# Hybrid recurrent and attention block: first projections taken from unnormalised x, and the y projection put ahead of the gates in each step

## Chip, cores and metric

One core of a Trainium2 chip. The metric is the device time in microseconds (us), 1733.96 as the median of three runs of the kernel before (1733.42 to 1734.18). The profile is one further execution: its own time is 1732.49 and its span, first to last instruction, 1730.7. All times inside it are counted from the start of that span. PE is TensorE, ACT ScalarE, DVE VectorE, POOL GpSimd, SP the engine that issues the weight loads.

## What is computed

x is 1024 tokens of 1024 features in float32. The part that the change touches is this (the rest is attention, the gated merge, the output projection and a SwiGLU block):

```python
h = rms_norm(x, norm_pre_mix)                # x / deviation(token) * gain(feature)
lru_u, lru_y, q, k, v, ... = split(h @ w_in) # u and y are 1280 wide each
u = causal_depthwise_conv(lru_u, width=4) + conv_b
r = sigmoid(u_block @ w_rg + b_rg); i = sigmoid(u_block @ w_ig + b_ig)
a = exp(-8 * r * softplus(-lru_lambda)); b = sqrt(1 - a*a) * (i * u)
lru_h[t] = a[t] * lru_h[t-1] + b[t]          # a scan over time
lru_out = lru_h * gelu(lru_y)
```

## The kernel before

Everything lies transposed: features on the 128 partitions, tokens along the free axis. The tokens are done in two halves of 512 (h = 0, 1). A projection makes one output tile of 128 features x 512 tokens from 8 weight tiles; each operand is split in a high and a low part, and three matmuls of 512 columns per weight tile (hi*hi, hi*lo, lo*hi) are summed in a PSUM bank. Lines 424, 425 and 426 are these three in `project`, lines 486 to 488 the same in `head`. Weights come through a ring of four buffers: SP loads a block of four tiles (`load`), POOL splits it in high (L358) and low part (L361), PE uses it. SP may load a block when POOL has split the one four places earlier; POOL may split one when PE is done with the one four places earlier.

Each half starts with the recurrent stage, `recurrent(h)`, which each of PE, ACT and DVE runs as its own instruction stream, in the order written. The ten tiles j of u and y pass through it. Tiles 0 and 1 are projected in `head`. Then comes one step for each j from 2 to 9, with these parts:

- PE: the u projection of tile j into bank 0 (5.5 us of matmuls), the two gate products of tile j-2 into banks 4 and 5 (`gates`, 2 or 3 weight tiles each), the y projection of tile j into bank 2. Bank 0 is free when ACT has copied it out (`u_copied`), bank 2 when ACT has taken the gelu of the last one (`gelu_made`).
- ACT: `conv_in(j)` copies u out of PSUM and makes the first tap (L738 to L747); `lru_out_hi(j-3)` (L791); `gate_fns(j-2)`, two Tanh (L759, L761), an Exp (L766) and a Tanh (L768); `conv_hi(j)` (L752); `gate_root(j-2)`, a Sqrt (L774); `decay(j-2)` (L786); `gelu(j)` (L780). Gelu, Exp and Sqrt lie in three different function tables, and each change of table is an ACT_TABLE_LOAD.
- DVE: `conv(j)`, three multiply-adds (L1155); `lru_out_lo(j-3)` (L1191); `conv_lo(j)` (L1161), which waits for `conv_hi(j)`; then `recurrence(j-2)`: L1167, which waits for the second Tanh, L1170 and L1171, which wait for the Exp and the Sqrt, L1174, the scan L1178, L1182, and the product with gelu, L1185.

After step 9 comes `kvq`: the k projections with the gates of tiles 8 and 9 between them, v, and then the q projections, of which the third may not start before DVE has made the low part of the first (`q_lo`, L1255); DVE makes that after the recurrence of tile 9. In the first half all of this stands behind the start: x tiles are loaded, ACT squares them, DVE sums them (L1422), PE sums over partitions (L436), ACT takes the root, DVE inverts (L1410) and makes a diagonal, PE spreads it (L444), and DVE and ACT make the normalised tiles (`normalise`, L1134 and L1143). 24 turns of two warm-up matmuls (L670) stand ahead on PE. A constant of the recurrence is made by 17 small DVE instructions (`prepare`), between tile 1 and step 2. The order of ACT's instructions in a step is

```python
conv_in(h, j, n + 2, j % 4)
if j > 2:
    lru_out_hi(h, j - 3)
gate_fns(h, j - 2, n + 2)
conv_hi(h, j, j % 4)
gate_root(h, j - 2)
decay(h, j - 2)
gelu(h, j, n + 6, j % 4)
```

Of the kernel before, what the change touches and what calls it, by code (L numbers as in the profile page):

```python
# [65 lines left out]
L_STEP = UNIT + [2, 2] + UNIT + (UNIT + GATE + UNIT) * 3  # L66

L_TAIL = UNIT + [3, 3] + UNIT + [2, 2]
V_BLOCKS = [4, 4, 4, 4]
# [45 lines left out]
def build(nc, x_d, par_d, alibi_d, eye_d, w_d, x1_d, out_d):  # L115
    with ExitStack() as ctx:
# [56 lines left out]
        lru_lo = at("lru_lo", [P, KR, T], F32R)  # L173
        mg_hi = at("mg_hi", [P, KD, T], F32R, reg_b)
# [33 lines left out]
        BK_U, BK_Y = (0, 1), (2, 6)  # L208
# [6 lines left out]
        par_loaded = sem("par_loaded")  # L215
# [92 lines left out]
        def _(sp_eng):  # L308
            def load(dram, g, sizes, n):
                off = 0  # L310
                for b, size in enumerate(sizes):

                    wait_pos(sp_eng, w_lo_made, n + b - RING + 1)
                    sp_eng.dma_start(w_raw[:, b % RING, 0:size * P],
                                     dram[g, :, off:off + size * P]).then_inc(w_loaded[b % RING], 16)
                    off += size * P

            def stream(stages, bases):
                for name, sizes, groups in stages:
                    per = 1 if len(sizes) % RING == 0 else 2  # L320
                    sizes2, dram, base = sizes * per, w_d[name], bases[name]
                    n_it = groups // per
                    first = 1 if base == 0 else 0
                    if first:
                        load(dram, 0, sizes2, 0)
                    if n_it - first == 1:
                        load(dram, first, sizes2, base + first * len(sizes2))
                    elif n_it > first:
                        with sp_eng.Fori(first, n_it) as g:
                            load(dram, g, sizes2, g * len(sizes2) + base)  # L330
# [3 lines left out]
            sp_eng.dma_start(par[:], par_d).then_inc(par_loaded, 16)  # L334
            sp_eng.dma_start(eye[:], eye_d).then_inc(par_loaded, 16)
# [62 lines left out]
        def _(pe):  # L398
# [34 lines left out]
            def narrow_sum(part, start, stop):  # L433

                for m in range(T // P):
                    last = mm(ps[:, m, 0:2], part[:, m * P:(m + 1) * P], ones[:, 0:2],  # L436
# [20 lines left out]
            def gates(h, j, n, size, slot, q, first=None):  # L457
# [9 lines left out]
                if last_tile:  # L467
                    pe.wait_ge(r_made, J)
                    pe.wait_ge(i_made, J)
# [4 lines left out]
            def head(h, j, ready):  # L474

                n = BASE[h]["head"] + 4 * j
                wait_pos(pe, row_out, 2 * (BK_Y[j] + 1) * h)
                for b in range(2):
                    for u, bank in enumerate((BK_U[j], BK_Y[j])):
                        pe.wait_ge(w_lo_made, n + 2 * b + u + 1)  # L480
                        for q in range(4):
                            k, w = 4 * b + q, slice(q * P, (q + 1) * P)
                            if ready:
                                pe.wait_ge(h_lo_made, KD * h + k + 1)
                            s = 2 * b + u
                            mm(ps[:, bank, :], w_hi[:, s, w], h_hi[:, k, :], start=(k == 0), stop=False)  # L486
                            mm(ps[:, bank, :], w_hi[:, s, w], h_lo[:, k, :], start=False, stop=False)  # L487
                            last = mm(ps[:, bank, :], w_lo[:, s, w], h_hi[:, k, :], start=False,  # L488
                                      stop=(k == KD - 1))
                        last.then_inc(blocks_done, 1)  # L490

            def recurrent(h):
                for j in range(2):
                    head(h, j, j == 0)
                if h:
                    stat_sum(2)
                for j in range(2, KR):
                    n, slot = 6 * (j - 2) + BASE[h]["step"], 6 * (j - 2)
                    wait_pos(pe, u_copied, (j + KR * h) * 2)
                    project(0, n, slot, UNIT, h_hi, h_lo)  # L500
                    i = j - 2
                    if i in (0, 4):
                        gates(h, i, n + 2, 2, slot + 2, 0, [(i - (i > 0)) % 4, (i + (i == 0)) % 4])
                    else:
                        gates(h, i, n + 2, 3, slot + 2, i)
                    wait_pos(pe, gelu_made, j + KR * h)
                    project(2, n + 4, slot + 4, UNIT, h_hi, h_lo)
# [163 lines left out]
            pe.wait_ge(summed_0, KD - 1)  # L671
            narrow_sum(acc, True, True)
            spread_rstd(1)
            for h in range(HALVES):
                recurrent(h)
                kvq(h)
                pe.wait_ge(par_loaded, 32)
# [20 lines left out]
        def _(act):  # L698
# [17 lines left out]
            def narrow_deviation(n):  # L716
# [878 lines left out]
```

## Time and profile before

| | |
|---|---|
| median of three runs | 1733.96 us |
| the profiled execution, its time and its span | 1732.49 and 1730.7 us |
| PE busy | 1692.4 us, 98% of the span |
| POOL busy | 1320.2 us, 76% |
| DVE busy | 801.4 us, 46% |
| ACT busy | 561.0 us, 32% |
| TensorE clock granted, mean | 0.991 of full |

A matmul of 512 columns is shown with 0.39 us, but the next one starts 0.23 us later: matmuls are pipelined and their ends are modelled. So PE's waits are read in starts, not in busy time. Shares of the span are means over stages: DVE is at 46% over the span, while in the recurrent stage it hardly rests.

### The profile page before, as it was taken

Reading aid. Unit: us, or ns where it says so; the run is one execution under the profiler, and the core shown is the slowest. Engines: PE = TensorE matmul, PEld = TensorE weight load, DVE = VectorE, ACT = ScalarE, POOL = GpSimd, SP = SyncE. Lnnn points to the kernel's source line nnn. Section 1 sums busy time; section 2 is a strip of 40 time slices with the busy share of each in tenths; the row PEclk is TensorE's granted clock in tenths of the full one; section 3 lists DMA queues with packets and bytes.
Section 4 is the critical chain, followed back from the end, with each engine's and each line's share of the span. In section 5 each row is a group of like instructions: output and inputs, shape, how many; then the busy total and the mean of one; then the engine's idle time right before and its main releaser. Section 6 shows DMA issues by size and latency. Waiting matters only on the chain.

```text
span 1730.7 us, 26755 instructions
## 1 busy us (share of the span) xinstructions
PE 1692.4 (98%) x7676; PEld 1392.5 (80%) x7676; DVE 801.4 (46%) x878; ACT 561.0 (32%) x1034; POOL 1320.2 (76%) x1344
## 2 busy tenths in 40 slices
PE   8999999999999999999999999999999999999995
PEld 6787888888888878888888888888888888888884
DVE  5899736651277987766421733211611232111013
ACT  4577435442236765254422322111200211111000
POOL 5799966777788999777777877776777777666774
PEclk8999999999999999999999999999999999999997
DMA  4333332232343333422323434322433343224331
GB/s 142 102 88 89 116 98 85 79 98 94 108 128 106 90 89 108 155 75 76 96 94 103 140 130 143 109 96 93 137 100 95 111 143 132 94 95 141 96 97 60
DMA packets 111228, 183.15 MB, mean 106 GB/s; under 512 B 12352, under 2 KB 38208, under 8 KB 111168
## 3 DMA queue, kind: packets, MB, share of 16 engines
q1 hardware_dynamic: 97056, 156.15, 29.2%
q10 hardware_dynamic: 14112, 26.22, 4.5%
q8 instruction: 35, 0.57, 0.1%
q14 instruction: 25, 0.20, 0.0%
HBM read 173.94 MB, written 8.39 MB: 105 GB/s over the span
## 4 chain that ended last, share of the span: by engine, by line
PE 86%; issue 5%; POOL 4%; DVE 3%; ACT 1%; DMA 0%; POOLq 0%; ACTq 0%; SPq 0%; DVEq 0%
PE ps L426 27%; PE ps L425 26%; PE ps L424 26%; POOL w_hi L358 3%; POOL w_lo L361 1%; PE ps L486 1%; PE ps L565 1%; PE ps L487 1%; PE ps L488 1%; PE ps L555 0%; PE ps L557 0%; PE ps L556 0%; PE ps L580 0%; PE ps L579 0%; DVE rows L1482 0%
## 5 line engine op out<-in xcount | busy, mean ns | idle before, releaser
L361 POOL TENSOR_TENSOR w_lo<-w_raw,w_hi 128x512 fp32r<-128x512 f32 (+2 forms) x664 | 849.4, 1279 | 55.4
L358 POOL TENSOR_SCALAR w_hi<-w_raw 128x512 fp32r<-128x512 f32 (+2 forms) x664 | 466.5, 703 | 334.2 <-PE ps L426 261.1
L424 PE MATMUL ps<-h_hi,w_hi 128*128 128x512 f32 x1376 | 538.1, 391 | 9.9 <-POOL w_lo L361 7.5
L426 PE MATMUL ps<-h_hi,w_lo 128*128 128x512 f32 x1376 | 541.0, 393 | 0.0
L425 PE MATMUL ps<-h_lo,w_hi 128*128 128x512 f32 x1376 | 538.8, 392 | 0.0
L424 PEld LDWEIGHTS ps<-h_hi,w_hi 128*128 128x128 f32 x1376 | 258.4, 188 | 71.2 <-issue 6.4
L425 PEld LDWEIGHTS ps<-h_lo,w_hi 128*128 128x128 f32 x1376 | 258.4, 188 | 57.3
L426 PEld LDWEIGHTS ps<-h_hi,w_lo 128*128 128x128 f32 x1376 | 258.6, 188 | 54.3
L1122 DVE TENSOR_TENSOR acc<-acc,sq 128x512 f32<-128x512 f32 x55 | 66.3, 1206 | 226.7 <-ACT sq L969 201.7
L1447 DVE TENSOR_TENSOR tmp<-ps,tmp 128x512 f32<-128x512 f32 x44 | 30.4, 691 | 301.8 <-PE ps L426 301.8
L426 PE MATMUL ps<-f_hi,w_lo 128*128 128x512 f32 x352 | 138.7, 394 | 0.0
L425 PE MATMUL ps<-f_lo,w_hi 128*128 128x512 f32 x352 | 138.0, 392 | 0.0
L424 PE MATMUL ps<-f_hi,w_hi 128*128 128x512 f32 x352 | 136.6, 388 | 0.0
L1049 ACT ACTIVATE f_hi<-tmp 128x512 f32 (+1 forms) x44 | 27.8, 633 | 230.8 <-DVE tmp L1447 230.8
L969 ACT ACTIVATE sq<-ps 128x512 f32 (+1 forms) x32 | 19.1, 597 | 225.9 <-PE ps L426 208.0
L1155 DVE SCALAR_TENSOR_TENSOR uc<-u_raw,par,uc 128x512 f32<-128x512 f32 x60 | 71.9, 1199 | 17.9 <-ACT uc L747 16.4
L425 PEld LDWEIGHTS ps<-f_lo,w_hi 128*128 128x128 f32 x352 | 66.1, 188 | 15.5
L424 PEld LDWEIGHTS ps<-f_hi,w_hi 128*128 128x128 f32 x352 | 66.1, 188 | 14.8
L426 PEld LDWEIGHTS ps<-f_hi,w_lo 128*128 128x128 f32 x352 | 66.2, 188 | 13.1
L893 ACT ACTIVATE prob<-prob,stat 128x128 f32<-128x128 f32 x128 | 49.7, 389 | 63.1 <-DVE stat L1276 63.1
L1450 DVE TENSOR_TENSOR f_lo<-tmp,f_hi 128x512 f32 (+1 forms) x44 | 45.0, 1024 | 42.4 <-ACT f_hi L1049 42.4
L1046 ACT ACTIVATE tmp<-ps 128x512 f32<-128x512 f32 x44 | 26.3, 598 | 117.2 <-PE ps L426 117.1
(193 smaller groups left out, 2431.3 us busy)
## 6 DMA issues: line engine op xcount, KB each, us to landing
w_raw<-w_f SPq DMA_DIRECT2D x176, 256.0 KB, 3.0
w_raw<-w_step SPq DMA_DIRECT2D x64, 256.0 KB, 2.6
w_raw<-w_b SPq DMA_DIRECT2D x64, 256.0 KB, 3.0
w_raw<-w_d SPq DMA_DIRECT2D x64, 256.0 KB, 2.7
w_raw<-w_a SPq DMA_DIRECT2D x96, 128.0 KB, 2.0
xs<-x_t ACTq DMA_DIRECT2D x32, 256.0 KB, 3.4
w_raw<-w_q SPq DMA_DIRECT2D x32, 256.0 KB, 3.2
w_raw<-w_o SPq DMA_DIRECT2D x32, 256.0 KB, 3.0
```

The costliest lines, as they stand in the source:

```text
L358: nc.gpsimd.tensor_scalar(w_hi[:, s, w], w_raw[:, s, w], 1.0, 0.0, ALU.mult, ALU.add).then_inc(w_hi_made, 1)
L361: nc.gpsimd.tensor_tensor(w_lo[:, s, w], w_raw[:, s, w], rd(w_hi[:, s, w]), ALU.subtract).then_inc(w_lo_made, 1)
L424: mm(out, w_hi[:, s, w], x_hi, start=(k == 0), stop=False)
L425: mm(out, w_hi[:, s, w], x_lo, start=False, stop=False)
L426: last = mm(out, w_lo[:, s, w], x_hi, start=False, stop=(k == total - 1))
L893: fn(prob[:, i, :], prob[:, i, :], ACT.Exp, bias=stat[:, 2, i:i + 1], accum_out=stat[:, 3, i:i + 1]).then_inc(exped, 1)
L1046: fn(tmp[:, 0, :], ps[:, 0, :], ACT.Silu).then_inc(silu_made, 1)
L1049: fn(f_hi[:, bass.ds(t, 1), :], tmp[:, 1, :], ACT.Copy).then_inc(f_hi_made, 1)
L1122: tt(acc[:], acc[:], sq[:], ALU.add).then_inc(summed, 1)
L1155: stt(uc[:, q, :], u_raw[:, k:k + T], col("conv_w", j + KR * k), uc[:, q, :], ALU.mult, ALU.add).then_inc(taps, 1)
L1447: tt(tmp[:, 1, :], ps[:, 1, :], tmp[:, 0, :], ALU.mult).then_inc(f_made, 1)
L1450: tt(f_lo[:, bass.ds(t, 1), :], tmp[:, 1, :], rd(f_hi[:, bass.ds(t, 1), :]), ALU.subtract).then_inc(f_lo_made, 1)
```

## The change

1. At the start of the first half, `head` projects x times the gain (xg_hi, xg_lo), which ACT and DVE make as the x tiles land, instead of the normalised tiles. The statistics are taken beside it on PE (the narrow sum after the third block, the spreading after the fifth). The reciprocal deviation is multiplied into the results: DVE's `scale_u` and `scale_y` for tiles 0 and 1. The normalised tiles are made after that, for step 2 onwards.
2. The parameters are loaded first, the four first weight blocks between the x tiles, the identity matrix last. `prepare` moves into the start, in two parts.
3. In every step of both halves the y projection goes ahead of the gates, on PE and in the order of the weight blocks (`L_STEP`, `step_offsets`). ACT's order in a step becomes conv_in, lru_out_hi, conv_hi, gelu, gate_fns, gate_root, decay. DVE's order in a step stays.
4. The first step of a half waits for tile 0's copy only, since tile 1 lies in other banks; y of tile 1 of the first half goes to bank 3.

The core of the diff:

```diff
-L_STEP = UNIT + [2, 2] + UNIT + (UNIT + GATE + UNIT) * 3
+L_STEP = UNIT + UNIT + [2, 2] + (UNIT + UNIT + GATE) * 3
...
-        BK_U, BK_Y = (0, 1), (2, 6)
+        BK_U, BK_Y = (0, 1), ((2, 3), (2, 6))
...
+            sp_eng.dma_start(par[:], par_d).then_inc(par_loaded, 16)
             for t in range(KD):
                 sp_eng.dma_start(rows[:, t, :], x_d[0][t]).then_inc(x0_loaded[t], 16)
-            sp_eng.dma_start(par[:], par_d).then_inc(par_loaded, 16)
-            sp_eng.dma_start(eye[:], eye_d).then_inc(par_loaded, 16)
+                if t in (0, 1, 3, 4):
+                    b = (0, 1, 3, 4).index(t)
+                    sp_eng.dma_start(w_raw[:, b, :], w_d["head"][0, :, b * CAP:(b + 1) * CAP])\
+                        .then_inc(w_loaded[b], 16)
+            sp_eng.dma_start(eye[:], eye_d).then_inc(eye_loaded, 16)
...
                         last.then_inc(blocks_done, 1)
+                        if h == 0 and u == 0 and (j, b) == (0, 1):
+                            pe.wait_ge(summed_0, KD - 1)
+                            narrow_sum(acc, True, True, 4)
+                        if h == 0 and u == 0 and (j, b) == (1, 0):
+                            spread_rstd(1)
...
-                    wait_pos(pe, u_copied, (j + KR * h) * 2)
-                    project(0, n, slot, UNIT, h_hi, h_lo)
+                    first = j == 2
+                    pe.wait_ge(u_copied, (j - first + KR * h) * 2)
+                    project(0, n, slot, UNIT, h_hi, h_lo, (h_lo_made, 0) if first and h == 0 else None)
+                    if first and h == 0:
+                        pe.wait_ge(y_scaled, 1)
+                    else:
+                        pe.wait_ge(gelu_made, j - first + KR * h)
+                    project(2, n + 2, slot + 2, UNIT, h_hi, h_lo)
                     i = j - 2
                     if i in (0, 4):
-                        gates(h, i, n + 2, 2, slot + 2, 0, [(i - (i > 0)) % 4, (i + (i == 0)) % 4])
+                        gates(h, i, n + 4, 2, slot + 4, 0, [(i - (i > 0)) % 4, (i + (i == 0)) % 4])
                     else:
-                        gates(h, i, n + 2, 3, slot + 2, i)
-                    wait_pos(pe, gelu_made, j + KR * h)
-                    project(2, n + 4, slot + 4, UNIT, h_hi, h_lo)
+                        gates(h, i, n + 4, 3, slot + 4, i)
...
+            def conv_scaled(j):
+                wait_pos(act, taps, j * 3)
+                fn(u_raw[:, 0:TAPS - 1], u_carry[:, bass.ds(j, 1), :], ACT.Copy).then_inc(u_ctx, 1)
+                act.wait_ge(u_copied, j * 2 + 1)
+                act.wait_ge(u_ctx, j + 1)
+                fn(u_carry[:, bass.ds(j, 1), :], u_raw[:, T:T + TAPS - 1], ACT.Copy)\
+                    .then_inc(u_copied, 1)
+                fn(uc[:, j, :], u_raw[:, 0:T], ACT.Identity, bias=col("conv_b", j),
+                   scale=col("conv_w", j)).then_inc(tap0, 1)
...
                     if j > 2:
                         lru_out_hi(h, j - 3)
-                    gate_fns(h, j - 2, n + 2)
                     conv_hi(h, j, j % 4)
+                    gelu(h, j, n + 4, j % 4)
+                    gate_fns(h, j - 2, n + 4)
                     gate_root(h, j - 2)
                     decay(h, j - 2)
-                    gelu(h, j, n + 6, j % 4)
...
+            for t in range(KD):
+                act.wait_ge(x0_loaded[t], 16)
+                fn(xg_hi[:, t, :], rows[:, t, :], ACT.Copy, scale=col("g_pre_mix", t))\
+                    .then_inc(xg_hi_made, 1)
+                fn(x1_all[:, t, :], rows[:, t, :], ACT.Square).then_inc(squared, 1)
...
+            def scale_u(j):
+                dve.wait_ge(blocks_done, 4 * j + 3)
+                wait_pos(dve, taps, j * 3)
+                wait_pos(dve, u_copied, j * 2)
+                tt(u_raw[:, TAPS - 1:], ps[:, BK_U[j], :], rstd_b[:], ALU.mult).then_inc(u_copied, 1)
+
+            def scale_y(j):
+                dve.wait_ge(blocks_done, 4 * j + 4)
+                tt(gy[:, j, :], ps[:, BK_Y[0][j], :], rstd_b[:], ALU.mult).then_inc(y_scaled, 1)
...
+            prepare(0)
+            dve.wait_ge(eye_loaded, 16)
             narrow_invert(0)
-            dve.wait_ge(spread, 1)
+            prepare(1)
+            dve.wait_ge(rstd_kept, 1)
+            scale_u(0)
+            scale_y(0)
             normalise(0, "g_pre_mix", ps[:, BK_RSTD, :], lambda t: rows[:, t, :], lambda t: (x0_loaded[t], 16))
```

## Rows read from the trace of the kernel before

**Rows 1.** The page's first part: busy time, share of the span and instructions.

```profile
PE 1692.4 (98%) x7676; PEld 1392.5 (80%) x7676; DVE 801.4 (46%) x878; ACT 561.0 (32%) x1034; POOL 1320.2 (76%) x1344
```

**Rows 2.** PE's waits: who waited for whom; us in total, times, longest.

```profile
PE ps L424 <- POOL w_lo L361: 7.5, 7, 2.6
...
PE ps L424 <- ACT gy L780: 1.5, 1, 1.5
```

**Rows 3.** PE in time order (start, us, line, [idle before]): third q projection.

```profile
210.34 0.49 PE L424 MATMUL ps<-h_hi,w_hi 128*128 128x512 f32 x1 [2.49 <-POOL w_lo L361]
...
688.84 0.50 PE L424 MATMUL ps<-h_hi,w_hi 128*128 128x512 f32 x1 [2.55 <-POOL w_lo L361]
```

**Rows 4.** DVE in time order: where the steps' chain starts, waits, ends.

```profile
59.57 1.75 DVE L1155 SCALAR_TENSOR_TENSOR uc<-u_raw,par,uc 128x512 f32<-128x512 f32 x2 [0.59 <-ACT uc L747]
...
174.51 0.95 DVE L1185 TENSOR_TENSOR g_h<-g_h,gy 128x512 f32<-128x512 f32 x1
...
183.70 1.38 DVE L1170 SCALAR_TENSOR_TENSOR g_r<-g_a,g_r 128x512 f32<-128x512 f32 x1 [3.43 <-ACT g_s L774]
...
209.52 0.69 DVE L1255 TENSOR_TENSOR q_lo<-ps,q_hi 128x512 f32 x1
...
534.74 1.77 DVE L1155 SCALAR_TENSOR_TENSOR uc<-u_raw,par,uc 128x512 f32<-128x512 f32 x2
...
652.89 0.96 DVE L1185 TENSOR_TENSOR g_h<-g_h,gy 128x512 f32<-128x512 f32 x1
```

**Rows 5.** Windows, the steps: length, busy (x) PE PEld DVE ACT POOL, clock, DMA.

```profile
59.57:175.46 115.89, 112.99 (x489) 90.95 (x488) 109.89 (x96) 85.24 (x123) 107.39 (x86) 1.00 0.32 89
...
534.74:653.85 119.11, 117.74 (x510) 95.04 (x509) 109.87 (x96) 86.58 (x126) 115.36 (x92) 1.00 0.32 90
```

**Rows 6.** DVE in time order, parts of one step (86.44 to 101.47).

```profile
86.44 4.52 DVE L1155 SCALAR_TENSOR_TENSOR uc<-u_raw,par,uc 128x512 f32<-128x512 f32 x3
...
90.88 0.99 DVE L1191 TENSOR_TENSOR lru_lo<-g_h,lru_hi 128x512 fp32r<-128x512 f32 x1
...
94.12 1.50 DVE L1170 SCALAR_TENSOR_TENSOR g_r<-g_a,g_r 128x512 f32<-128x512 f32 x1
...
101.47 1.09 DVE L1155 SCALAR_TENSOR_TENSOR uc<-u_raw,par,uc 128x512 f32<-128x512 f32 x1
```

**Rows 7.** ACT in time order, the same step.

```profile
87.18 0.67 ACT L759 ACTIVATE g_r<-ps,half_b 128x512 f32<-128x512 f32 x1
...
91.17 0.62 ACT L752 ACTIVATE uc_hi<-uc 128x512 fp32r<-128x512 f32 x1
...
93.10 0.64 ACT L774 ACTIVATE g_s<-g_r 128x512 f32<-128x512 f32 x1
...
97.32 1.28 ACT L780 ACT_TABLE_LOAD   x1
...
99.11 0.20 ACT L738 ACTIVATE u_raw<-u_carry 128x3 f32<-128x3 f32 x1
```

**Rows 8.** DVE in time order where POOL leaves it alone most.

```profile
32.51 2.76 DVE L1155 SCALAR_TENSOR_TENSOR uc<-u_raw,par,uc 128x512 f32<-128x512 f32 x3 [3.19 <-ACT uc L747]
...
586.11 0.88 DVE L1170 SCALAR_TENSOR_TENSOR g_r<-g_a,g_r 128x512 f32<-128x512 f32 x1
...
591.01 0.69 DVE L1185 TENSOR_TENSOR g_h<-g_h,gy 128x512 f32<-128x512 f32 x1
```

**Rows 9.** Time order, start: warm-up on PE, first and last normalising on DVE.

```profile
1.92 9.46 PE L670 MATMUL ps<-ones 128*128 128x128 f32 x48 [1.92 <-POOL v_hl L349]
...
15.58 1.41 DVE L1134 SCALAR_TENSOR_TENSOR tmp<-rows,par,ps 128x512 f32<-128x512 f32 x2 [1.57 <-PE ps L444]
...
27.33 1.99 DVE L1143 TENSOR_TENSOR h_lo<-tmp,h_hi 128x512 fp32r<-128x512 f32 x2
```

**Rows 10.** Windows of the start, columns as in rows 5.

```profile
14.70:24.90 10.20, 6.59 (x14) 3.54 (x13) 8.79 (x11) 3.54 (x6) 5.30 (x5) 0.50 0.37 133
...
24.90:43.90 19.00, 19.00 (x84) 15.58 (x84) 8.28 (x11) 7.16 (x14) 14.47 (x14) 1.00 0.26 70
```

More of the change, by code:

```diff
@@ L64, with step_offsets @@
 L_HEAD = UNIT + UNIT
-L_STEP = UNIT + [2, 2] + UNIT + (UNIT + GATE + UNIT) * 3
+L_STEP = UNIT + UNIT + [2, 2] + (UNIT + UNIT + GATE) * 3
 L_TAIL = UNIT + [3, 3] + UNIT + [2, 2]
+def step_offsets():
+    out, at = [], 0
+    for g in (2, 3, 3, 3):
+        y = at + (8 + 2 * g) * P
+        out += [at, at + CAP, y, y + CAP, at + 8 * P, at + (8 + g) * P]
+        at = y + 8 * P
+    return out
+OFFSETS = {"step": step_offsets()}
 V_BLOCKS = [4, 4, 4, 4]
@@ L308, in _, with load @@
         def _(sp_eng):
-            def load(dram, g, sizes, n):
-                off = 0
+            def load(dram, g, sizes, n, offsets=None):
+                end = 0
                 for b, size in enumerate(sizes):
+                    off = offsets[b] if offsets else end
                     wait_pos(sp_eng, w_lo_made, n + b - RING + 1)
@@ L315, in load @@
                                      dram[g, :, off:off + size * P]).then_inc(w_loaded[b % RING], 16)
-                    off += size * P
+                    end = off + size * P
             def stream(stages, bases):
@@ L431, in project, with narrow_sum @@
                         inner()
-            def narrow_sum(part, start, stop):
+            def narrow_sum(part, start, stop, bank=0):
                 for m in range(T // P):
-                    last = mm(ps[:, m, 0:2], part[:, m * P:(m + 1) * P], ones[:, 0:2],
+                    last = mm(ps[:, bank + m, 0:2], part[:, m * P:(m + 1) * P], ones[:, 0:2],
                               start=start, stop=stop)
@@ L472, in gates, with head @@
                     project(4 + g, n + g, slot + g, [size], uc_hi, uc_lo, tiles=tiles)
-            def head(h, j, ready):
+            def head(h, j):
                 n = BASE[h]["head"] + 4 * j
-                wait_pos(pe, row_out, 2 * (BK_Y[j] + 1) * h)
+                hi, lo = (h_hi, h_lo) if h else (xg_hi, xg_lo)
+                wait_pos(pe, row_out, 2 * (BK_Y[h][j] + 1) * h)
                 for b in range(2):
-                    for u, bank in enumerate((BK_U[j], BK_Y[j])):
+                    for u, bank in enumerate((BK_U[j], BK_Y[h][j])):
                         pe.wait_ge(w_lo_made, n + 2 * b + u + 1)
@@ L714, in acc_hi, with narrow_deviation @@
                 fn(acc_hi_of(n)[:], acc[:], ACT.Copy).then_inc(acc_hi_made, 1)
-            def narrow_deviation(n):
+            def narrow_deviation(n, bank=0):
                 act.wait_ge(stat_mm, n + 1)
-                fn(dev.rearrange("p (m o) -> p m o", o=1), ps[:, 0:4, 0:1], ACT.Sqrt, bias=eps_ap,
+                fn(dev.rearrange("p (m o) -> p m o", o=1), ps[:, bank:bank + 4, 0:1], ACT.Sqrt, bias=eps_ap,
                    scale=1.0 / D).then_inc(dev_made, 1)
@@ L795, in recurrent @@
                     done = BASE[h]["head"] + 4 * j
-                    conv_in(h, j, done + 3, j, BK_U[j])
-                    conv_hi(h, j, j)
-                    gelu(h, j, done + 4, j, BK_Y[j])
+                    if h:
+                        conv_in(h, j, done + 3, j, BK_U[j])
+                        conv_hi(h, j, j)
+                        gelu(h, j, done + 4, j, BK_Y[h][j])
+                    else:
+                        conv_scaled(j)
+                        conv_hi(h, j, j)
+                        act.wait_ge(y_scaled, j + 1)
+                        fn(gy[:, j, :], gy[:, j, :], ACT.Gelu_apprx_tanh).then_inc(gelu_made, 1)
                 if h:
@@ L1195, in recurrent @@
                 for j in range(2):
+                    if h == 0 and j:
+                        scale_u(j)
                     conv(h, j, j)
@@ L1201, in recurrent @@
                 else:
-                    prepare()
+                    scale_y(1)
                 open_sum(1 + 2 * h)
```

107 lines of the change are left out of this document (54 added, 53 removed).

## The prediction, made before the changed kernel was built or run

> **What bounds the kernel now.** I read the busy times first: PE is busy for 98% of the span [rows 1], so an edit can bring only what PE waits, or cost what it makes PE wait. Then the list of PE's waits: it gives POOL the most, 7.5 us in seven waits, and gelu 1.5 [rows 2]. The largest two of the seven are 2.49 and 2.55 us, both at the third q projection [rows 3], and POOL is named there wrongly. The code lets that projection start only after DVE's first q_lo, and that ends at 209.52 + 0.69 = 210.21, right before PE's 210.34 [rows 3, 4]. So at the end of the recurrent stage of each half PE does not set the time: the chain through ACT and DVE does. I write M7 for the end of the product with gelu in step 9: 174.51 + 0.95 = 175.46, and 652.89 + 0.96 = 653.85 in the second half [rows 4]. PE starts the third q projection 34.9 and 35.0 us after M7 [rows 3, 4]. Whatever moves M7 later moves all that follows.
>
> Third, the windows over the steps. From conv(2) on DVE (59.57 and 534.74) to M7 there are eight turns: 115.9/8 = 14.49 us a turn in the first half, 119.1/8 = 14.89 in the second [rows 4, 5]. DVE is busy for 109.9 of these, 95% and 92%; POOL for 107.4 and 115.4. DVE's 46% of the whole span hides that. A turn costs PE 22 weight tiles at most, 66 matmuls; 84 matmuls take 19.00 us when dense [rows 10], so 0.226 each and 14.9 a turn. PE, DVE and POOL are within 7% of each other here, and a longer turn of any of them is paid at once.
>
> Last, one turn in time order. On DVE: conv from 86.44 to 90.96, then lru_lo, conv_lo and L1167, then from 94.12 on L1170 to L1185, and the next conv at 101.47 [rows 6]. On ACT: gate functions from 87.18, conv_hi at 91.17, the root ends at 93.74, gelu with its table load from 97.32 to 99.11, where the next work starts [rows 7]. The point is where they lie: the four gate functions (87.18 to 91.17, 3.99 us) run beside DVE's conv, and gelu (1.79 us) beside DVE's scan. Neither costs the turn anything.
>
> **The change, part by part.**
>
> *ACT's new order in a step.* gate_fns(j-2) and gelu(j) move behind conv_hi(j). conv_hi waits for all of DVE's conv(j), and DVE's L1170 waits for the root, which comes after the gate functions. So now they stand in one line: conv_hi 0.63 (91.17 up to the table load of the root at 91.80), gelu 1.79, gate functions 3.99, root 93.74 - 91.80 = 1.94, together 8.35, with handoffs 8.45 us [rows 7]. Between conv and L1170 lay 94.12 - 90.96 = 3.16 us before [rows 6]. The three table loads of a turn stay three. Behind the waiting ACT are decay and the next conv_in; behind the waiting DVE is the whole recurrence, and the next conv behind it in the same queue. Nothing breaks this loop: conv(j+1) follows recurrence(j-2) on DVE in program order. The trace of before shows the same wait once, where kvq puts the gate functions out of conv's cover: L1170 idles 3.43 us for g_s [rows 4].
>
> The turn L is thus conv + 8.45 + the stretch from L1170 to the next conv. With this turn's own lengths: 4.52 + 8.45 + 7.35 = 20.3 us [rows 6], my upper end. With the shortest of each in the trace, where POOL left DVE alone: conv 2.76, and 591.70 - 586.11 = 5.59, L = 16.8 [rows 8], my lower end. The mean turn of 14.49 with 8.45 in place of 3.16 gives 19.8, and a mean conv and stretch of 19.8 - 8.45 = 11.3. POOL's 107.4 us in eight turns are 13.4 a turn; that is 93% of 14.49 but 68% of some 19.8, and DVE's lengths follow POOL's presence. Between 8.35 (POOL absent) and 11.3 (93%) this gives 8.35 + 2.95 x 0.68/0.93 = 10.5, so L = 19.0 us, the value I take.
>
> PE's 14.9 us of a turn fit in 19.0: it will wait some 4 us in every turn, at the y projection, for the gelu of the step before, and POOL's splits and SP's loads wait behind PE. None of these three is late then.
>
> *y ahead of the gates on PE, in POOL's and SP's order.* The same blocks in another order, the same 66 matmuls: 0. It takes away the gelu wait (1.5 us) and gives uc_lo 5.5 us more, but that is PE's time, which no longer ends anything. The cover that made the moved work free was conv on DVE; that is the price above.
>
> *kvq.* After step 9, ACT has the gates of tile 8 without waiting for PE. Of M7 to the product of tile 8 (15.5 us before, product of tile 7 at 175.46, L1170 at 183.70 [rows 4]) I take off 1.4: from M7 the copy 0.7, a table load 1.3, four functions 2.7, the root 1.9 and handoffs give 6.8 to L1170, against 8.2. So PE's third q projection comes 33.5 us after M7.
>
> *The start.* Before, after the warm-up's end at 11.38 [rows 9], PE waits for the deviation and does 14 matmuls in 10.2 us at a clock of 0.50 (the level of 1.2 GHz; the engine had done little but wait before) [rows 10]. Now it goes on right away: 96 matmuls, 21.7 us at full clock, and about 2.5 us for the narrow sum and the spreading, to about 35.5 instead of 44: 8.5 us earlier. But the steps begin with the normalised tiles. Their making took 15.58 to 29.32, 13.7 us [rows 9]. It now starts after the spreading (about 26.7), a copy and two scalings of 0.7: at 29.2, and ends at 42.9. In DVE's queue conv(0) stands behind it. From there in one line: scaling, tap, conv 2.8, conv_hi and conv_lo 1.4 for tile 0, the same for tile 1, scale_y, five memsets: 15 us by lengths as in [rows 6 to 8], and conv(2) starts at 58 (55 to 61), where it was 59.57. So 8.5 us on PE become 1.6 on the chain. `prepare` was in the way of conv(2) and is gone from there; that is in it. The x tiles land later by four weight blocks between them, but the last is there long before PE's third block needs it: 0. PE waits at the gates of tile 0 for about 5 us.
>
> *Waits for tile 0's copy only, bank 3:* 0, hidden by the above.
>
> **Sum.** First half: M7 = 58 + 8 x 19.0 = 210.0, against 175.46: +34.5; less 1.4: +33.1. Second half: 8 x 19.0 = 152.0 against 119.1, less 1.4: +31.5 (its conv(2) waits for the inversion of the deviation, as before). Together +64.6. The profiled 1732.49 becomes 1797.1; the median of the runs is 1.5 higher, so 1799 us. Each us of L is 16 us of the result.
>
> By the ends of L: 16.8 gives 64.6 - 35.2 = +29.4, 1763; 20.3 gives +85.4, 1819.
>
> **A rule of the skill against a row.** ACT's table load takes 1.28 us, and its gelu begins 1.30 us after the load's start (97.32; the next work at 99.11 follows from it) [rows 7]. The Trainium skill, "ScalarE: Activation LUTs", section "What ACT_TABLE_LOAD costs", puts about 1.38 us of drain on top of each switch. By that the three switches in one line would make L about 4.1 us longer, an estimate from that page, and the result about 1865. The measured line has no such time in it, so it stands outside the sum.
>
> **The rivals.**
>
> *POOL lets go (1745 to 1780).* POOL is throttled by a waiting PE, and DVE's instructions fall to their quiet lengths: L is 16.0 to 17.8. For it: 2.76 against 4.52 us for the same conv [rows 6, 8]. Against it: POOL still has 22 tiles a turn, and PE frees its buffers after its wait, so that POOL's splits fall in DVE's long stretch. At L = 16.8: 1763. Chance 0.12. (The Trainium skill, "SBUF — State Buffer", section "SBUF: two separate sides", has the two take turns at a shared port pair for whole instructions. By that rule the quiet lengths need POOL truly absent, not merely less busy; the trace agrees in so far as the same three multiply-adds take 2.76 us beside an idle POOL and 4.52 beside a busy one [rows 6, 8].)
>
> *The clock falls in PE's waits (1805 to 1825).* At the start a clock of 0.50 lasted 10.2 us, 5.1 us of PE's work [rows 10]. With it in a turn PE needs 14.9 + 5.1 = 20.0, and PE becomes the bound of such turns, by 1 us each, at most +16: 1815. Against it: in the waits of 2.5 us at the q projections nothing like it is seen, and the windows over the steps read 1.00 [rows 5]. Chance 0.07.
>
> *ACT's order costs nothing, and it is faster (1728 to 1732).* If conv_hi did not wait for DVE's conv, or gate_fns were early enough, the turn would stay at 14.5 to 14.9. Then the sum is -1.6 - 1.4 - 1.4 = -4.4: 1729.6 by the median. It decides from L = 14.7 downward; at L of 15.0 the first half is already later. Even the quiet lengths give 16.8. Chance 0.06.
>
> *No change of the end (within 0.2%).* The change doesn't do to the end what it says: PE starts earlier and all is given back, with L = 15. Chance 0.03.
>
> **How the numbers follow.** The forecast, L between 17.8 and 20.3, has 0.72: 1799 us. The range for 8 in 10 takes in most of the first rival and half of the second: 1758 to 1818. 0.2% is 3.5 us, about what a measurement of this kernel can tell from no change. Slower has 0.72 + 0.12 + 0.07 = 0.91, same 0.03, faster 0.06.
>
> **What would show it.** In the changed kernel's trace: DVE's conv(j) to conv(j+1) about 19 us apart; ahead of L1170's successor a DVE wait of 3 us or more released by ACT's root, and one ahead of L1167's released by the second Tanh; ACT's table load for gelu right behind conv_hi; PE waiting some 4 us per turn ahead of the y projection, released by gelu; PE's first head matmul at 11.5 with the clock at full; conv(2) at 55 to 61; the third q projection 33.5 us after M7. It is wrong if the turns stay below 16 us, or if the waits of PE in the steps are released by POOL. If conv(2) comes before 50, the start was mis-sized.

## The result, and the profile after

The changed kernel takes 1802.62 us as the median of six runs (1799.86 to 1805.10), the kernel before 1734.07 beside it. The ratio is 1.0395, with an interval of 1.0382 to 1.0409. The forecast was 1799 us. The profiled execution took 1805.1 us, 72.6 more than that of before.

The page's first part, the granted clock in 40 slices, and the shares of the chain that ended last; then the same shares of the kernel before:

```profile
PE 1715.8 (95%) x7676; PEld 1409.3 (78%) x7676; DVE 798.2 (44%) x890; ACT 564.7 (31%) x1040; POOL 1305.0 (72%) x1344
...
PEclk8999999999999999999999999999999999999998
...
PE 76%; DVE 11%; ACT 8%; issue 4%; POOL 1%; DMA 0%; DVEq 0%; ACTq 0%; SPq 0%; POOLq 0%
```
```profile
PE 86%; issue 5%; POOL 4%; DVE 3%; ACT 1%; DMA 0%; POOLq 0%; ACTq 0%; SPq 0%; DVEq 0%
```

PE has the same 7676 matmuls and falls from 98% to 95% of the span [rows 1]: it waits more. These are its waits (us in total, times, longest), to be read against [rows 2]:

```profile
PE ps L446 <- ACT gy L819: 30.3, 12, 3.9
PE ps L446 <- ACT g_i L800: 14.4, 4, 6.0
PE ps L446 <- ACT u_carry L767: 6.5, 1, 6.5
PE ps L446 <- POOL w_lo L383: 6.2, 2, 3.1
...
PE ps L508 <- DVE xg_lo L1479: 3.0, 3, 1.7
```

L446 to L448 are the three matmuls of `project` and `gates`, L819 is gelu, L798 and L800 are the two Tanh, and L767 belongs to ACT's copy of u for the tiles 0 and 1. The windows over the steps, from conv(2) to M7, with the columns of [rows 5]:

```profile
64.00:217.26 153.26, 130.16 (x524) 103.55 (x523) 105.87 (x96) 85.88 (x123) 114.41 (x99) 0.93 0.26 76
575.31:729.21 153.90, 131.09 (x530) 104.11 (x529) 104.69 (x96) 87.91 (x126) 114.62 (x100) 0.93 0.26 75
```

A turn is 153.3/8 = 19.16 us and 153.9/8 = 19.24, against 14.49 and 14.89. DVE is busy for 106 and 105 us of the eight turns, 4 to 5 less than before. That was 92 to 95% of the time before and is 69 and 68% now. What it waits for stands in one turn of the time order, first ACT's, then DVE's (start, us, line; idle before and its releaser in brackets):

```profile
86.58 0.63 ACT L791 ACTIVATE uc_hi<-uc 128x512 fp32r<-128x512 f32 x1 [3.71 <-DVE uc L1202]
87.22 1.28 ACT L819 ACT_TABLE_LOAD   x1
88.52 0.60 ACT L819 ACTIVATE gy<-ps 128x512 f32<-128x512 f32 x1
89.01 0.68 ACT L798 ACTIVATE g_r<-ps,half_b 128x512 f32<-128x512 f32 x1
...
93.13 1.28 ACT L813 ACT_TABLE_LOAD   x1
94.42 0.63 ACT L813 ACTIVATE g_s<-g_r 128x512 f32<-128x512 f32 x1
```
```profile
90.31 0.69 DVE L1226 SCALAR_TENSOR_TENSOR g_i<-g_i,uc 128x512 f32<-128x512 f32 x1 [1.45 <-ACT g_i L800]
95.16 1.36 DVE L1229 SCALAR_TENSOR_TENSOR g_r<-g_a,g_r 128x512 f32<-128x512 f32 x1 [4.16 <-ACT g_s L813]
...
101.41 4.52 DVE L1202 SCALAR_TENSOR_TENSOR uc<-u_raw,par,uc 128x512 f32<-128x512 f32 x3
...
114.55 1.18 DVE L1229 SCALAR_TENSOR_TENSOR g_r<-g_a,g_r 128x512 f32<-128x512 f32 x1 [4.16 <-ACT g_s L813]
...
120.61 1.79 DVE L1202 SCALAR_TENSOR_TENSOR uc<-u_raw,par,uc 128x512 f32<-128x512 f32 x1
```

The line of the forecast is here: DVE's conv (L1202) ends at about 86.54, ACT makes uc_hi, loads gelu's table, makes gelu, the gate functions and the root, and DVE's L1229 (the L1170 of before) starts at 95.16, 8.62 us after conv's end. That distance is 8.62 in fifteen of the sixteen turns. In the first one it is 7.20: there the function before gelu is the gelu of tile 1, and ACT loads no table for it. DVE rests twice in a turn's distance, 1.45 and 4.16 us.

The third q projection, where the chain releases PE:

```profile
248.89 0.50 PE L446 MATMUL ps<-h_hi,w_hi 128*128 128x512 f32 x1 [3.12 <-POOL w_lo L383]
```

It stood at 210.34 before [rows 3], so the first half costs 38.5 us. In the second half it stands at 760.80, where it was 688.84: another 33.4. Together 72.0 of the 72.6.

### The profile page after: what moved, and what is told of

It reads as the page before. It is cut to its first block, busy times and chain, and to the rows that moved or that the text cites. A ratio compares the mean times of both kernels' runs of the same rounds, so it can differ in the third digit from the quotient of the medians.

```text
span 1803.2 us, 26791 instructions
## 1 busy us (share of the span) xinstructions
PE 1715.8 (95%) x7676; PEld 1409.3 (78%) x7676; DVE 798.2 (44%) x890; ACT 564.7 (31%) x1040; POOL 1305.0 (72%) x1344
## 4 chain that ended last, share of the span: by engine, by line
PE 76%; DVE 11%; ACT 8%; issue 4%; POOL 1%; DMA 0%; DVEq 0%; ACTq 0%; SPq 0%; POOLq 0%
PE ps L447 23%; PE ps L448 23%; PE ps L446 23%; DVE uc L1202 4%; DVE g_h L1237 2%; ACT L813 1%; ACT L805 1%; DVE g_s L1230 1%; ACT L819 1%; DVE g_i L1233 1%; PE ps L596 1%; DVE g_h L1244 1%; ACT g_a L805 1%; ACT g_r L807 1%; ACT g_r L798 1%
## 5 line engine op out<-in xcount | busy, mean ns | idle before, releaser
L380 POOL TENSOR_SCALAR w_hi<-w_raw 128x512 fp32r<-128x512 f32 (+2 forms) x664 | 456.0, 687 | 422.5 <-PE ps L448 306.1
L446 PE MATMUL ps<-h_hi,w_hi 128*128 128x512 f32 x1376 | 545.9, 397 | 46.7 <-ACT gy L819 30.3
L448 PE MATMUL ps<-h_hi,w_lo 128*128 128x512 f32 x1376 | 546.7, 397 | 0.0
L447 PE MATMUL ps<-h_lo,w_hi 128*128 128x512 f32 x1376 | 546.2, 397 | 0.0
L446 PEld LDWEIGHTS ps<-h_hi,w_hi 128*128 128x128 f32 x1376 | 262.9, 191 | 112.2 <-ACT gy L819 35.5
L447 PEld LDWEIGHTS ps<-h_lo,w_hi 128*128 128x128 f32 x1376 | 262.5, 191 | 57.9
L448 PEld LDWEIGHTS ps<-h_hi,w_lo 128*128 128x128 f32 x1376 | 262.7, 191 | 55.8
L1169 DVE TENSOR_TENSOR acc<-acc,sq 128x512 f32<-128x512 f32 x55 | 66.8, 1214 | 226.3 <-ACT sq L1009 201.7
L448 PE MATMUL ps<-f_hi,w_lo 128*128 128x512 f32 x352 | 138.7, 394 | 0.0
L446 PE MATMUL ps<-f_hi,w_hi 128*128 128x512 f32 x352 | 136.6, 388 | 0.0
L1202 DVE SCALAR_TENSOR_TENSOR uc<-u_raw,par,uc 128x512 f32<-128x512 f32 x60 | 76.1, 1268 | 9.6 <-ACT uc L786 6.1
L446 PEld LDWEIGHTS ps<-f_hi,w_hi 128*128 128x128 f32 x352 | 66.1, 188 | 14.8
L448 PEld LDWEIGHTS ps<-f_hi,w_lo 128*128 128x128 f32 x352 | 66.2, 188 | 13.1
```

The costliest lines, as they stand in the source:

```text
L380: nc.gpsimd.tensor_scalar(w_hi[:, s, w], w_raw[:, s, w], 1.0, 0.0, ALU.mult, ALU.add).then_inc(w_hi_made, 1)
L446: mm(out, w_hi[:, s, w], x_hi, start=(k == 0), stop=False)
L447: mm(out, w_hi[:, s, w], x_lo, start=False, stop=False)
L448: last = mm(out, w_lo[:, s, w], x_hi, start=False, stop=(k == total - 1))
L1169: tt(acc[:], acc[:], sq[:], ALU.add).then_inc(summed, 1)
L1202: stt(uc[:, q, :], u_raw[:, k:k + T], col("conv_w", j + KR * k), uc[:, q, :], ALU.mult, ALU.add).then_inc(taps, 1)
```

## The experiments

A turn is the time from conv(j) to conv(j+1) on DVE. Each ratio is to the kernel before, in runs on the same chip. e1 and e2 were executed once, so they have a time and no interval; their differences of 54 and 61 us are far above the 5 us over which the six runs of the changed kernel spread.

### The changed kernel with ACT's old order (e1)

```diff
-                    conv_hi(h, j, j % 4)
-                    gelu(h, j, n + 4, j % 4)
                     gate_fns(h, j - 2, n + 4)
+                    conv_hi(h, j, j % 4)
                     gate_root(h, j - 2)
                     decay(h, j - 2)
+                    gelu(h, j, n + 4, j % 4)
```

> The changed kernel with ACT's order in a step put back (gate functions ahead of conv_hi, gelu last); y stays ahead of the gates on PE. Theory (ACT's line conv_hi, gelu, gate functions, root alone makes the turn of 19.2): with that order back and nothing else in the way the turn would be 14.5 to 15, and the time about 1738. Refined theory (each order has its own loop): gelu of step j-1 is then last on ACT, y of step j on PE waits for it, since both use bank 2, and the gates come after y; so 5.5 (y) + 4.1 (gates) + 4.0 (gate functions) + 0.6 (conv_hi) + 1.9 (root) + 2.2 (L1229, L1230) + 0.6 (decay) + 1.8 (gelu) + handoffs = 21 us a turn, and about 1829. Rival (DVE's and POOL's sharing sets the turn, order plays no part): no change, 1802.

Measured: 1856.75 us, turns of 22.3 and 22.4 us in the mean of a half, and up to 23.5. So ACT's new order is not a mistake that could just be undone. ACT first, then PE, in one turn:

```profile
111.28 0.69 ACT L798 ACTIVATE g_r<-ps,half_b 128x512 f32<-128x512 f32 x1 [10.35 <-PE ps L448]
...
122.46 0.80 PE L446 MATMUL ps<-h_hi,w_hi 128*128 128x512 f32 x1 [5.80 <-ACT gy L819]
```

ACT's gate functions wait 10 us for PE's gates, which now stand behind y; PE's y waits for bank 2, which the gelu of the step before frees, and ACT makes that last. It is a second loop, through one PSUM bank. The turn is longer than I had worked out (21 us, for 1829). The clock falls to 0.50 for 6.8 us behind each of these 6-us waits, which can take up to 3.4 us of PE's work in a turn. That is enough for the difference; how much of it is due to the clock was not separated.

### The kernel before with ACT's new order alone (e2)

```diff
-                    gate_fns(h, j - 2, n + 2)
                     conv_hi(h, j, j % 4)
+                    gelu(h, j, n + 6, j % 4)
+                    gate_fns(h, j - 2, n + 2)
                     gate_root(h, j - 2)
                     decay(h, j - 2)
-                    gelu(h, j, n + 6, j % 4)
```

(The new order no longer implies that the last gates have been read, so PE's gates also wait for the gate functions of the tile before.)

> The kernel before with only ACT's order in a step changed (conv_hi, gelu, gate functions, root, decay); PE's order, the blocks and the start stay. PE gets the two explicit waits for r and i ahead of the gates, as in the changed kernel, since the order no longer implies them. Theory (ACT's line makes the turn): 19.2 us a turn, conv(2) still at 59.6, DVE's wait for the root about 4.2 us, time about 1800. Rival (PE's order, y ahead of the gates, makes the loss; ACT's order is harmless): turns of 14.5 to 15 and about 1734.

Measured: 1795.22 us, turns of 18.82 and 18.90. A turn late in the first half has the same wait of DVE as the changed kernel (L1169 is the L1170 of before):

```profile
204.53 1.08 DVE L1169 SCALAR_TENSOR_TENSOR g_r<-g_a,g_r 128x512 f32<-128x512 f32 x1 [4.16 <-ACT g_s L773]
```

With PE's, POOL's and SP's order as before, three lines of ACT's stream alone cost 61 us. This is the main cause. e4 below adds PE's and the weight blocks' order to it and takes the same time (1795.5): y ahead of the gates is worth nothing there.

### The start alone, and the steps alone (e3, e4)

e3 is the changed kernel with the step order of before on PE, ACT and in the weight blocks. e4 is the kernel before with the changed step order on all of them.

```diff
-L_STEP = UNIT + UNIT + [2, 2] + (UNIT + UNIT + GATE) * 3
+L_STEP = UNIT + [2, 2] + UNIT + (UNIT + GATE + UNIT) * 3
...
+                    gate_fns(h, j - 2, n + 2)
                     conv_hi(h, j, j % 4)
-                    gelu(h, j, n + 4, j % 4)
-                    gate_fns(h, j - 2, n + 4)
```

> The changed kernel's start (projections on unnormalised x, load order, early preparation) with the steps of the kernel before, on PE, ACT and in the weight stream. Theory (the chain through ACT and DVE sets the end of the stage): only conv(2)'s start counts, 64.0 against 59.6, so +4.4: 1738 (1736 to 1740). Rival (PE's earlier head is worth something): 1726 to 1730.

> The kernel before with only the changed steps (block order, PE, ACT), its start as before. Theory: 1802.6 less the 4.4 of the start: 1798 (1795 to 1801), turns of 19.2. Rival (start and steps act on each other, as by a clock that falls at the start): within 1 us of 1802.

Measured: e3 1741.68 us, ratio 1.0044 (1.0030 to 1.0058); e4 1795.51 us, ratio 1.0358 (1.0342 to 1.0374). So the steps cost 3.6%, and the start costs too, 0.4% by itself and 1802.6 - 1795.5 = 7.1 us on top of the steps. A part of the 7.1 is a gain in e4: its conv(2) comes at 55.62, 4 us ahead of that of the kernel before, since `prepare`'s 17 instructions take 5.0 us there, with fewer and shorter splits of POOL's beside them, and not 9.7.

e3 is above its expectation, which had counted conv(2)'s delay alone. PE in e3, its two long waits where the steps begin:

```profile
47.93 0.80 PE L446 MATMUL ps<-h_hi,w_hi 128*128 128x512 f32 x1 [5.72 <-ACT u_carry L767]
...
59.47 0.65 PE L446 MATMUL ps<-uc_hi,w_hi 128*128 128x512 f32 x1 [3.46 <-DVE uc_lo L1220]
```

conv(2) comes at 62.69 (59.57 before [rows 4]), and the first gates at 59.47, which started at 49.78 before. From there PE is the bound, and the third q projection of the first half is 8.8 us late (219.12 against 210.34). Behind the wait at that projection the clock reads 0.50 for 3.4 us, which it does not in the kernel before, and conv(2) of the second half is 10.3 us late. In the second half nothing more than 0.2 us is lost.

### A second bank for y (e5), and with ACT's old order (e6)

```diff
-                        pe.wait_ge(gelu_made, j - first + KR * h)
-                    project(2, n + 2, slot + 2, UNIT, h_hi, h_lo)
+                        pe.wait_ge(gelu_made, j - 1 + KR * h)
+                    project(2 + 4 * (j % 2), n + 2, slot + 2, UNIT, h_hi, h_lo)
...
-                    gelu(h, j, n + 4, j % 4)
+                    gelu(h, j, n + 4, j % 4, 2 + 4 * (j % 2))
```

> The changed kernel with y of the steps going to banks 2 and 6 in turn, so that PE's y projection waits for the gelu of two steps before; nothing else. Theory (the loop through ACT and DVE sets the turn, PE's wait for gelu is only where PE's spare time shows): the 30 us of waits for gelu vanish from PE's list and come back under other names, turns stay 19.2, time 1799 to 1804. Rival (PE's wait for the single y bank is the cost, as PE's list of waits has it on top): at least those 30 us go, about 1772 or less.

Measured: 1786.34 us, ratio 1.0308 (1.0292 to 1.0323), between the two expectations, of which neither was met. PE's waits for gelu are gone (30.3 us to nothing), and those for ACT's copy of u in the steps grow from 3.6 to 22.2 us. conv's end to L1229 stays 8.62, again in fifteen of sixteen turns. But the turns fall to 18.09 and 18.29, for DVE's conv is shorter: 3.25 us in the mean of the sixteen turns, where it was 4.15. That is 14.4 of the 16.3 us won. In this run its length goes by what POOL does meanwhile: 2.32 us in the five turns in which POOL is busy for 0.5 us of it or less, 4.51 in the two in which it is busy for 4.4. One of the short ones:

```profile
100.13 2.32 DVE L1202 SCALAR_TENSOR_TENSOR uc<-u_raw,par,uc 128x512 f32<-128x512 f32 x3
```

So PE's wait for gelu was mostly a symptom, which came back under another name, but taking it away also moved POOL's splits away from conv, and that I had not foreseen.

e6 is e5 with the order of e1 on ACT.

> The kernel of the two y banks with ACT's order in a step put back as well (gate functions ahead of conv_hi, gelu last). Theory: the loop of the run with the order back and one bank (22.3 us a turn: gelu, y, gates, gate functions) is cut by the second bank, and conv covers the gate functions again, so turns of 14.9 to 15.4, the matmuls' own time; with the changed start that is 1738 to 1743, near the start-only run. Rival (y ahead of the gates is itself bad, as ACT gets the gates 5.5 us later): turns of 17 and more, 1765 or more.

Measured: 1747.45 us, ratio 1.0080 (1.0066 to 1.0093), turns of 15.30 and 15.50. So both loops are needed for a full account: with two banks the old order of ACT is worth 39 us, where with one bank it cost 54. And y ahead of the gates brings nothing even then: e6 is 6 us behind e3, which has the gates first, and above its expectation. In the first turn of the second half ACT waits 6.6 us for PE's gates, which stand behind y, and conv's end to L1229 is 7.6 us, where e3 has 2.9.

### Gelu's table load taken out of the line (e7)

```diff
-                    gelu(h, j, n + 4, j % 4)
+                    gelu(h, j, n + 4, j % 4, f=ACT.Copy)
```

> The changed kernel with a Copy in place of the Gelu in the steps (the gelu of tiles 2 to 9 is left out; the instruction's place, operands and length of 0.60 us stay). Copy needs no table of its own, so one of three table loads of 1.28 us per turn leaves ACT's line. Theory (each us in ACT's line is a us of the turn): turns of 17.9, and 16 x 1.28 = 20.5 us less, 1782. Rival (the turn is set by DVE's and POOL's sharing or by PE's clock): 1800 to 1803.

Measured: 1782.43 us, ratio 1.0281 (1.0262 to 1.0300). DVE's waits in a turn (compare the 4.16 above):

```profile
129.52 1.13 DVE L1229 SCALAR_TENSOR_TENSOR g_r<-g_a,g_r 128x512 f32<-128x512 f32 x1 [2.73 <-ACT g_s L813]
```

conv's end to L1229 is 7.19, 1.43 less than 8.62, and the turns are 1.2 and 1.7 us shorter. What ACT saves between conv_hi and the root is paid back at once and nearly in full: 20.2 us, where fifteen turns save 1.43 each (21.5; the first turn had no load to save). A switch of table is priced by this too, and a second time by the first turn of the changed kernel, which is 1.42 shorter in the same place: one load of 1.28 and its handoffs, and nothing on top.

### Less of POOL's work (e10)

```diff
                     pool.wait_ge(w_hi_made, n + b + 1)
+                    if part:
+                        w = slice(0, P)
                     nc.gpsimd.tensor_tensor(w_lo[:, s, w], w_raw[:, s, w], rd(w_hi[:, s, w]),
```

> The changed kernel with POOL's low parts of the weights made for the first of each block's tiles only, in the step stage alone (left out: the other tiles' low parts, whose old contents PE multiplies instead). POOL's work falls by over a third there; ACT's line stays. Theory (L is ACT's line of 8.6 plus DVE's parts, whose lengths follow POOL's presence): turns between the quiet 16.0 (2.33 + 8.62 + 5.03) and 18, time 1751 to 1783. Rival (POOL has nothing to do with DVE's lengths): turns of 19.2, 1802.

Measured: 1766.17 us, ratio 1.0192 (1.0176 to 1.0207). The windows from conv(2) to M7, columns as above, and DVE in one turn (L1204 is the L1202 of the changed kernel, L1231 its L1229):

```profile
58.63:194.66 136.03, 124.13 (x526) 99.54 (x525) 83.44 (x96) 85.90 (x123) 77.46 (x99) 0.97 0.30 87
551.93:689.53 137.60, 125.31 (x535) 101.04 (x534) 82.81 (x96) 87.91 (x126) 75.59 (x100) 0.98 0.30 85
```
```profile
124.36 2.65 DVE L1204 SCALAR_TENSOR_TENSOR uc<-u_raw,par,uc 128x512 f32<-128x512 f32 x3
...
135.63 1.12 DVE L1231 SCALAR_TENSOR_TENSOR g_r<-g_a,g_r 128x512 f32<-128x512 f32 x1 [4.16 <-ACT g_s L815]
```

DVE has the same 96 instructions and is busy for 83.4 us instead of 105.9. conv falls from 4.52 to 2.65, ACT's line stays 8.62, and the turns are 17.0 and 17.2. That DVE's lengths follow POOL's work is shown. POOL was still busy for 57% of the stage. By the interpolation of the forecast the turn would then be 8.62 + 8.35 + 2.95 x 0.57/0.93 = 18.8; it is 17.0, about the forecast's lower end with its quiet lengths. So POOL's share of busy time is a poor measure of what it costs DVE. The forecast's own lower end says the same: in the kernel before POOL was busy for 5.34 of the 5.59 us from 586.11 on, which stood there as quiet lengths [rows 8]. Which of the two kinds of split (the rounding with one operand, the difference with two) does the stretching was not separated.

### What can be kept of the change (e8, e9)

e8 is the kernel before with `prepare` moved forward, on DVE to behind the normalising and on ACT to behind the first deviation, and nothing else.

```diff
-                else:
-                    prepare()
...
+            prepare()
```

> The kernel before with one edit of the change alone: the 17 small DVE instructions and the two of ACT that make the recurrence's constant move from between tile 1 and step 2 to the start (ACT's behind the deviation, DVE's behind the normalising). Theory: conv(2) on DVE starts at 51 to 53 instead of 59.6, PE no longer waits for ACT's copy and gelu at 58 to 70, the matmuls become the bound from the first step, and 3 to 5 us are won: 1729 to 1731. Rival (POOL's splitting gives it back, as DVE's work now falls in with it): within 1.5 us of 1734.

Measured: 1730.99 us, ratio 0.9985 (0.9976 to 0.9994). conv(2) starts at 52.81, 6.8 us earlier, and the third q projection only 0.9 earlier: the turns are 15.2 us in the mean, near PE's own 14.9, and PE no longer waits for ACT in them. The profiled executions differ by 1.5 us only, where the medians differ by 3.3; that of the kernel before is among its faster ones.

e9 adds to it what bounds the end of the recurrent stage. ACT makes the keys behind the decay of the last tiles, and the high part of v before the output of tile 9; DVE takes v ahead of the low output of tile 9, so that q_lo comes earlier.

```diff
-                        keys(0, NCH * h)
...
-                lru_out_hi(h, 9)
...
+                keys(0, NCH * h)
...
+                lru_out_hi(h, 9)
...
-                lru_out_lo(h, 9)
                 values(0)
                 values(1)
+                lru_out_lo(h, 9)
```

> The kernel before with the early preparation and a shorter tail: behind the steps, ACT's copy of the first keys (0.8 us) and of v (1.2 us) move out of the line between the product of tile 9 and the first q_lo, and DVE makes v's low part ahead of the last lru_lo. Theory (the third q projection waits for this line alone): the way from M7 to it shortens from 35.0 to 33, PE's two waits of 2.7 us there to 0.7, so 4 us less than the early preparation's 1731.0: 1727 (1726 to 1729). Rival (POOL or the blocks are late there too): within 1 us of 1731.

Measured: 1725.81 us, ratio 0.9958 (0.9945 to 0.9972), faster than both kernels and just below the expected range. q_lo is ready 31.7 us after M7 instead of 34.75, and the list of PE's waits, against [rows 2]:

```profile
PE ps L424 <- POOL w_lo L361: 4.2, 9, 0.8
PE ps L486 <- DVE h_lo L1140: 3.2, 2, 2.5
```

In the first row the two waits of 2.5 us are gone (longest 0.8); the 2.5 of the second row is a wait for the normalised tiles in `head`, which the edit does not touch. Against its own runs of the kernel before e8 wins 3.3 us and e9 7.8, so 4.5 lie between them, and two times 2.5 is 5.0. That also settles that they were waits for q_lo and not for POOL's w_lo, under whose name they stood: POOL's work is as it was. In the traces PE gains 2.7 and 2.8 us on e8 at the two places. And counted off by tiles, POOL's low part of the block with which this projection starts ended at 205.44 in the kernel before, 4.9 us before PE started.

## Why the prediction was right, and where its steps were off

The time of 1799 us was 3.6 off, and the cause of nearly all of it is the one named: ACT's gate functions and gelu lost DVE's conv as their cover, and the turn is a loop through two in-order queues. e2 shows it by doing that alone, e7 by shortening it. By the steps of the sum:

| step | predicted | measured |
|---|---|---|
| conv(2), first half | -1.6 (58) | +4.4 (64.0) |
| eight turns, first half | +36.1 (19.0 each) | +37.4 (19.16) |
| M7 to the third q | -1.4 | -3.3 |
| start of the second half | 0 | +2.0 |
| eight turns, second half | +32.9 | +34.8 (19.24) |
| M7 to the third q | -1.4 | -3.4 |
| sum | +64.6 | +71.9 |

The sum is 7.3 us short, twice what the median shows. The measured column comes from the two profiled executions; that of the changed kernel is the slowest of its six, and that of the kernel before is one of its faster ones. So 3.6 flatters the working a little.

**ACT's line.** 8.45 predicted, 8.62 measured. Working it out from one turn's rows of before held to 0.17 us.

**DVE's share of the turn.** 10.5 predicted; 19.16 and 19.24 less the mean line (8.44 and 8.62) leave 10.7 and 10.6. The value held, its reason did not. I had taken 3.16 us, the gap of one turn, for the gap of all, and so a conv and stretch of 11.3 for before. The sixteen gaps of before (2.86 to 5.27) have means of 3.70 and 4.22, and 14.49 and 14.89 less these leave 10.8 and 10.7. So DVE's instructions became hardly shorter, although POOL's share fell from 93 and 97% to 75%; I had a base 0.5 us too high and took 0.8 off it for POOL. Two errors of a like size cancelled, which was luck. The same interpolation missed e10 by 1.8 us. Its lower end was misread too. POOL was not absent in [rows 8], nor idle as the passage on the first rival has it: it was busy for 1.93 us of the conv of 2.76, and conv takes 2.34 elsewhere in the kernel before (at 43.52) and 2.33 in e1 with POOL idle. And 5.59 reaches only to the end of the product; the next conv starts 6.16 us after L1170. With 2.34 and 6.16 the lower end is 16.95, by chance near the 16.8.

**The start, mis-sized.** "8.5 us on PE become 1.6 on the chain" was wrong in its sign: conv(2) is 4.4 us later. Two terms failed.

First, the pace of the head matmuls. I had put DVE's low part and its sum of squares per x tile at their quiet lengths. Beside POOL's splits they are these, the quiet pair below them:

```profile
12.01 1.78 DVE L1479 SCALAR_TENSOR_TENSOR xg_lo<-rows,par,xg_hi 128x512 fp32r<-128x512 f32 x1
13.72 1.09 DVE L1485 TENSOR_TENSOR acc<-acc,x_all 128x512 f32<-128x512 f32 x1
...
22.44 0.74 DVE L1479 SCALAR_TENSOR_TENSOR xg_lo<-rows,par,xg_hi 128x512 fp32r<-128x512 f32 x1
23.11 0.68 DVE L1485 TENSOR_TENSOR acc<-acc,x_all 128x512 f32<-128x512 f32 x1
```

That is 2.7 us a tile, where PE needs 6 matmuls or 1.4. PE starts at 11.29, as forecast, and then waits for xg_lo three times, and its clock falls. The window, columns as before:

```profile
21.10:31.30 10.20, 9.33 (x26) 7.55 (x27) 6.33 (x23) 0.17 (x1) 2.15 (x3) 0.50 0.32 103
```

So the clock of 0.50 that the change meant to leave is met a little later, this time with 26 matmuls in it. The spreading ends at 35.2 instead of 26.7, the normalising runs from 37.15 instead of 29.2 to 50.35 instead of 42.9, and the head ends at 43.3, 1.0 us before that of the kernel before and not 8.5.

Second, a wait that I did not see. conv(0)'s copy on ACT stands behind all of ACT's share of the normalising, and u(2) on PE waits for it:

```profile
50.01 0.79 PE L446 MATMUL ps<-h_hi,w_hi 128*128 128x512 f32 x1 [6.55 <-ACT u_carry L767]
```

The 5 us that I had PE wait at the gates of tile 0 are not there; this wait stands in their place. e3 shows the two together: from the first gates at 59.47 PE is the bound. The last term, 15 us from the last normalised tile to conv(2), was 13.6 (50.35 to 63.99).

**After M7, mis-sized.** 31.6 us against 33.5 predicted, in both halves. The product of tile 8 follows that of tile 7 by 13.9 us, not 14.1, and that of tile 9 that of tile 8 by 14.1, where I had left 15.0: I gave the gain of the ready gates to tile 8 alone. From there to the third q projection it is 3.65 us, where it was 4.35; this last 0.7 was not followed up.

**The start of the second half.** I took it as unchanged; it is 2.0 us later. The clock reads 0.50 for 3.4 us behind the wait at the third q projection, 1.7 us of PE's work; e3, which has such a fall too, loses 1.6 us in the same stretch. The other 0.3 stays open.

**The rivals.** POOL did not let go: conv is 4.52 again in the turn shown. e10, which takes a third of its busy time away, gives a turn of that rival's size (17.0). The clock did fall in PE's waits, in eleven places from conv(2) to the third q projection of the two halves, nine of them in the windows over the steps, which read 0.93; but the turns with a fall are no longer than those without, since PE had 4 us of room a turn. A dense turn is 14.9 us, and PE's waits and its slow stretches fill the rest. In e1 PE is in the loop and has no such room, so there a fall can cost time. That ACT's order costs nothing was excluded by e2. The drain at a table switch, by which the result would have been 1865, is refuted: gelu starts at 88.52, 1.30 us after the start of its load, and e7 saves 1.43 us a turn for one load, not 2.7.

Of the signs named ahead three were not as said: conv(2) at 64.0 lies outside the 55 to 61, the third q projection follows M7 by 31.6, and PE's waits for gelu are twelve of 2.5 us in the mean, not one of 4 in every turn. The other signs were found.

## What to carry to other kernels

In queues that run in order, an instruction moved a few places can lose the work that covered it; before you move one, ask what each engine does at that moment and whether the instruction it now stands behind waits for another engine. The price of a broken cover can be summed from rows of one turn to within some per cent, while an engine's 44% of busy time says nothing of it. If a wait goes away and most of the time stays, look for the loop, since two queues that wait for each other pass the wait on (e5), and a buffer and an order can each hide the other's fault (e1, e6).

## What was not expected of the hardware

**Small DVE instructions are stretched too.** Seven instructions on 128x10 elements, of the kernel before beside POOL's splits and of the changed kernel with POOL idle:

```profile
50.31 4.15 DVE L1400 SCALAR_TENSOR_TENSOR sp<-sp 128x10 f32<-128x10 f32 x7
```
```profile
27.56 1.39 DVE L1458 SCALAR_TENSOR_TENSOR sp<-sp 128x10 f32<-128x10 f32 x7
```

4.15 us against 1.39. One by one, the three of the seven that start between two instructions of POOL's take 0.17 us, and the four that start during one take 0.54 to 1.15 and end within 0.05 us of its end. conv's large ones take 0.98 to 1.79 in the turn from 86.44 on, and 0.75 with POOL idle (e1). So a tiny instruction waits about as long for POOL as a large one does. By the Trainium skill, "SBUF — State Buffer", section "SBUF: two separate sides", the two take turns at a shared port pair for whole instructions, and this agrees: 2.8 us more over seven instructions, beside which POOL ran five.

**The clock falls after short waits.** In the changed kernel, from the steps on, it went to 0.50 for 3.4 us at six gaps of 2.5 to 3.5 us between matmul starts, and for 6.8 us at the two of 6.4; of three gaps of 4.2 to 4.3 us it fell for 3.4 us at two and for 6.8 at one. But four gaps of 2.5 to 2.8 us in the same run had no fall with them, nor had the two of 2.9 and 3.0 us at the third q projection in the kernel before. What separates these cases was not tested.

**Matmul starts.** In e3 dense matmuls start 233 ns apart from 60 to about 190 us and 229 ns apart after; in e10 it is 233 until about 110 us, and in e4 for some 20 us. Elsewhere in the recurrent stages it is mostly 229. In e3 this is about 2 us over the stage, and its cause stays open.
